# Residual additions inside the next stage, two weight units fed per chunk, and sums of squares in three column tiles

## The reference

```python
h = x
f = _swiglu(_rmsnorm(h, ffn1_pre_g), ...)
h = h + 0.5 * _rmsnorm(f, ffn1_post_g)
u = _rmsnorm(h, mix_pre_g)
c_q, c_kv, k_pe, rw, gates = split(u @ w_in)
...                                   # attention and RWKV-7, merged into mix
h = h + _rmsnorm(mix @ w_out, mix_post_g)
f = _swiglu(_rmsnorm(h, ffn2_pre_g), ...)
h = h + 0.5 * _rmsnorm(f, ffn2_post_g)
gp = sigmoid(_rmsnorm(h, ple_pre_g) @ w_ple_gate)
h = h + _rmsnorm(gp * (pemb @ w_ple_proj), ple_post_g)
```

## Time and profile before

| | |
|---|---|
| median of three runs | 3861.78 us (3854.52 to 3871.53) |
| the profiled execution | 3863.07 us, of which the span of the trace is 3861.3 us |
| TensorE products busy | 3430.6 us, 89% of the span |
| VectorE, ScalarE, GpSimd busy | 1695.9, 929.8, 440.8 us |
| mean granted TensorE clock | 0.932 of full speed |

### The profile page before, as it was taken

One profiled execution on the slowest core, in us unless ns is written; L12 is line 12 of the kernel. 1 busy time (PEld: TensorE's weight loads), 2 busy tenths in 40 slices (PEclk: granted clock), 3 DMA queues, 4 the chain that ended last, 5 costly groups with the idle time before them and its releaser, 6 DMA issues. The chain is left out here.

```text
span 3861.3 us, 69674 instructions
## 1 busy us (share of the span) xinstructions
PE 3430.6 (89%) x28907; PEld 3086.5 (80%) x28907; DVE 1695.9 (44%) x2998; ACT 929.8 (24%) x1610; POOL 440.8 (11%) x457
## 2 busy tenths in 40 slices
PE   7999999969999799889994888869869999999776
PEld 6999999959999637766662767659859999999766
DVE  3343343353121245345444777755154443343443
ACT  3111111121000105434441333333221111111131
POOL 0000000020000000033331344420010000000212
PEclk9999999979999898989996899979979999999878
DMA  2011111122222300056552011023121111111122
GB/s 102 34 55 45 50 39 45 44 107 75 91 94 94 110 2 13 16 206 208 191 192 60 14 31 31 12 95 117 67 83 50 50 50 33 50 50 39 75 80 97
DMA packets 114583, 279.64 MB, mean 72 GB/s; under 512 B 45428, under 2 KB 56500, under 8 KB 113236
## 3 DMA queue, kind: packets, MB, share of 16 engines
q1 hardware_dynamic: 95860, 199.87, 15.4%
q0 software_dynamic: 18432, 75.51, 5.6%
HBM read 231.41 MB, written 43.80 MB: 71 GB/s over the span
## 5 line engine op out<-in xcount | busy, mean ns | idle before, releaser
L79 PE MATMUL f_psg<-f_u_hi,f_w_hi 128*128 128x352 f32 x1056 | 347.1, 329 | 62.7 <-DVE f_w_lo L336 58.2
L428 DVE TENSOR_TENSOR c_x<-c_x,f_psd 128x352 f32<-128x352 f32 x480 | 246.2, 519 | 318.0 <-PE f_psd L81 318.0
L79 PE MATMUL f_psd<-f_hid_hi,f_w_hi 128*128 128x352 f32 x1056 | 350.3, 332 | 18.2 <-DVE c_x L428 9.8
L332 ACT ACTIVATE f_w_hi<-f_raw 128x1024 fp32r<-128x1024 f32 x132 | 136.6, 1054 | 915.7 <-PE f_psd L81 352.3
L79 PE MATMUL f_psu<-f_u_hi,f_w_hi 128*128 128x352 f32 x1056 | 342.5, 324 | 5.5 <-DVE f_w_lo L336 5.5
L80 PE MATMUL f_psg<-f_u_lo,f_w_hi 128*128 128x352 f32 x1056 | 342.7, 325 | 0.0
L81 PE MATMUL f_psg<-f_u_hi,f_w_lo 128*128 128x352 f32 x1056 | 342.5, 324 | 0.0
L80 PE MATMUL f_psd<-f_hid_lo,f_w_hi 128*128 128x352 f32 x1056 | 341.6, 324 | 0.0
L81 PE MATMUL f_psd<-f_hid_hi,f_w_lo 128*128 128x352 f32 x1056 | 341.3, 323 | 0.0
L80 PE MATMUL f_psu<-f_u_lo,f_w_hi 128*128 128x352 f32 x1056 | 340.2, 322 | 0.0
L81 PE MATMUL f_psu<-f_u_hi,f_w_lo 128*128 128x352 f32 x1056 | 339.8, 322 | 0.0
(11 more groups left out here) (391 smaller groups left out, 7226.3 us busy)
## 6 DMA issues: line engine op xcount, KB each, us to landing
f_raw<-in_ffn_gu SPq DMA_DIRECT2D x88, 512.0 KB, 4.3
f_raw<-in_ffn_d SPq DMA_DIRECT2D x44, 512.0 KB, 4.0
proj<-in_out SPq DMA_DIRECT2D x36, 528.0 KB, 2.9
inw_raw<-in_w_in_units SPq DMA_DIRECT2D x36, 512.0 KB, 3.9
h<-c_x SPq DMA_DIRECT2D x24, 528.0 KB, 2.7
r_old<-h SPq DMA_DIRECT2D x3, 4224.0 KB, 12.9
c_x<-proj SPq DMA_DIRECT2D x16, 528.0 KB, 4.5
mgw_raw<-in_merge_units SPq DMA_DIRECT2D x16, 512.0 KB, 4.7
```

What stands on the lines that cost most here:

```text
L79: pe.matmul(out, w_hi, x_hi, start=start, stop=False)
L332: act.activation(w_hi[:, u % 3, :], raw[:, u % 3, :], ACT.Copy).then_inc(hi_done, 1)
L428: dve.tensor_tensor(a, a, ps_d[:, n % 2, 0:TB], ALU.add).then_inc(added, 1)
```

## The change

The stages r1, r2 and r3 are gone. What they did is written into the beginning of the stage that follows (`Residual`, `WideNorm`); r4 stays as `last_residual_phase`.

- **Old h by chunk.** SP loads old h in chunks of 528 KB into a ring of three buffers, stores chunk c of the sum when it is added, and loads chunk c + 3 behind that store. In f2 and in the input projection the first two weight units are loaded ahead of this, in the embedding unit 0.
- **By chunk on VectorE**: scale chunk c + 1 (and add old h, for chunks 0, 2, 4, 6, 7; in the embedding 0, 1, 2, 4, 6, 7), then u_lo of chunk c. GpSimd adds the others.
- **Two units per chunk.** In f1, f2 and the input projection TensorE takes, for each chunk, the 9 products of unit 0 and the 9 of unit 1 into six banks. In the embedding it takes the three blocks of unit 0 per chunk, after the products with p for these blocks.
- **Sums of squares.** In the five norms of f1, in, f2, pl and r2's squares, each chunk's squares go from ScalarE to TensorE, which multiplies them with 32 columns of ones, one token block to each of three column tiles (output partitions 0, 32, 64). The residual norms whose squares were summed before have one such product of `n_total`. The root and the reciprocal are then 96 x 352, and each block's row is spread by a product with a contraction of one.

The diff, cut to its core:

```diff
+class WideNorm:
+    def act_square(self, act, x, c):
+        wait(act, self.sq_summed, c - 1)
+        act.activation(self.buf.sq[:, c % 2, :], x[:, c, :], ACT.Square).then_inc(self.sq_ready, 1)
+    def pe_sum(self, pe, bank, c):
+        pe.wait_ge(self.sq_ready, c + 1)
+        for b in range(NTB):
+            mm = pe.matmul(bank[32 * b:32 * (b + 1), 0:TB], self.env.ones[:, 0:32],
+                           self.buf.sq[:, c % 2, token_block(b)], start=c == 0, stop=c == KC - 1)
+        mm.then_inc(self.sq_summed, 1)
...
+    def pe_spread(self, pe, banks):
+        pe.wait_ge(self.rs_ready, 1)
+        for b in range(NTB):
+            if b >= len(banks):
+                pe.wait_ge(self.rb_ready, b - len(banks) + 1)
+            pe.matmul(banks[b % len(banks)][:, 0:TB], self.env.ones[32 * b:32 * b + 1, :],
+                      self.buf.rs[32 * b:32 * b + 1, :], start=True, stop=True).then_inc(self.spread, 1)
...
+class Residual:
+    RING = 3
...
+    def sp_all(self, sp):
+        for c in range(self.RING):
+            self.sp_load(sp, c)
+        for c in range(KC):
+            self.sp_store(sp, c)
+            if c + self.RING < KC:
+                self.sp_load(sp, c + self.RING)
...
 def ffn_phase(...):                   # ScalarE
+            split_hi(act, 0, 0)
+            for c in range(KC):
+                x_in(act, c)
+                act_hi(act, x, g_col, u_hi, c, u_hi_ready)
+                if c == 0:
+                    split_hi(act, 0, 1)
+                norm.act_square(act, x, c)
             norm.act_root(act, ps_d[:, 1, :])
             norm.act_rb(act, nbanks)
...
 def input_projection_phase(...):      # VectorE
+            res.dve_gain(dve)
+            res_norm.dve_reciprocal(dve)
+            dve.wait_ge(res_norm.rb_ready, NTB)
+            res.dve_scale(dve, 0, buf.rb[:, :])
+            wu.split_lo(dve, 0, 0)
+            for c in range(KC):
+                if c < KC - 1:
+                    res.dve_scale(dve, c + 1, buf.rb[:, :])
+                res.wait_chunk(dve, c)
+                dve_lo(dve, x, g_col, u_hi, u_lo, c, u_hi_ready, u_lo_ready)
+                if c == 0:
+                    wu.split_lo(dve, 0, 1)
+            norm.dve_reciprocal(dve)
...
 def embedding_phase(...):             # ScalarE, then TensorE
+            res_norm.act_root(act, psn[:, 1, :])
+            res_norm.act_rb(act, nbanks)
+            act.wait_ge(p_in, 16)
+            act.activation(p_hi[:, :, :], pe_in[:, :, :], ACT.Copy).then_inc(p_hi_ready, 1)
+            wu.split_hi(act, 0, 0)
...
+            wu.ready(pe, 0, 0)
+            pe.wait_ge(p_lo_ready, 1)
+            for b in range(NTB):
+                wu.product(pe, ps[:, b, 1, 0:TB], 0, KC, PC, p_hi, p_lo, token_block(b))
...
-def residual_phase(nc, env, name, x, g_col, coef, res, h_out, buf, stored, summed, last=False):
+def last_residual_phase(nc, env, name, x, g_col, coef, res, h_out, buf, stored):
-        BY_POOL = (0, 2, 4, 6)
+        BY_POOL = (1, 3, 5)
-            sp.dma_start(old[:, :, :], res).then_inc(old_in, 16)
             for c in range(KC):
+                sp.dma_start(old[:, c, :], res[:, c, :]).then_inc(old_in[c], 16)
...
-            norm.pe_sums(pe, ps_sum)
-            norm.pe_spread_all(pe, ps_rb)
+            norm.pe_total(pe, ps_sum)
+            norm.pe_spread(pe, [ps_rb[:, b, :] for b in range(NTB)])
```

More of the change, by code:

```diff
@@ L387, in _ @@
         def _(dve):
[L388 to L392, removed]
+            if res is not None:
+                res.dve_gain(dve)
+                res_norm.dve_reciprocal(dve)
+                dve.wait_ge(res_norm.rb_ready, NTB)
+                res.dve_scale(dve, 0, buf.rb[:, :])
+            split_lo(dve, 0, 0)
+            for c in range(KC):
+                if res is not None and c < KC - 1:
+                    res.dve_scale(dve, c + 1, buf.rb[:, :])
+                x_in(dve, c)
+                dve_lo(dve, x, g_col, u_hi, u_lo, c, u_hi_ready, u_lo_ready)
+                if c == 0:
+                    split_lo(dve, 0, 1)
+            norm.dve_reciprocal(dve)
+            rb3 = buf.rb[:, :].rearrange("p (b t) -> p b t", b=NTB)
             def gate_evac(s, j):
@@ L559, in ready, with product @@
         pe.wait_ge(self.lo_done, i * 2 + (k + 1))
-    def product(self, pe, out, k, first, chunks, x_hi, x_lo, tokens, x_ready=None):
+    def product(self, pe, out, k, first, chunks, x_hi, x_lo, tokens):
         for c in range(chunks):
-            if x_ready is not None:
-                pe.wait_ge(x_ready, c + 1)
             w = slice((first + c) * P, (first + c + 1) * P)
@@ L615, in _ @@
                 sp.wait_ge(stored[k], 16 * (N_IN // 2))
-            sp.wait_ge(*reading)
+            sp.wait_ge(res.stored, 16 * KC)
+        @block.gpsimd
+        def _(pool):
+            res.pool_adds(pool)
         @block.scalar
         def _(act):
[L620 to L623, removed]
+            res_norm.act_root(act, psn[:, 1, :])
+            res_norm.act_rb(act, nbanks)
+            wu.split_hi(act, 0, 0)
+            for c in range(KC):
+                res.wait_chunk(act, c)
+                act_hi(act, x, g_col, u_hi, c, u_hi_ready)
+                if c == 0:
+                    wu.split_hi(act, 0, 1)
+                norm.act_square(act, x, c)
             norm.act_root(act, psn[:, 1, :])
@@ L631, in _ @@
         def _(dve):
[L632 to L637, removed]
+            res.dve_gain(dve)
+            res_norm.dve_reciprocal(dve)
+            dve.wait_ge(res_norm.rb_ready, NTB)
+            res.dve_scale(dve, 0, buf.rb[:, :])
+            wu.split_lo(dve, 0, 0)
+            for c in range(KC):
+                if c < KC - 1:
+                    res.dve_scale(dve, c + 1, buf.rb[:, :])
+                res.wait_chunk(dve, c)
+                dve_lo(dve, x, g_col, u_hi, u_lo, c, u_hi_ready, u_lo_ready)
+                if c == 0:
+                    wu.split_lo(dve, 0, 1)
+            norm.dve_reciprocal(dve)
+            dve.wait_ge(norm.rb_ready, NTB)
             def evac(i, k):
```

320 lines of the change are left out of this document (226 added, 94 removed).

## The result

The changed kernel takes 3803.73 us, the median of four runs (3791.69 to 3810.84), against 3860.45 for the kernel before (four runs, 3854.52 to 3871.53): a ratio of 0.9847, with an interval of 0.9811 to 0.9883. The forecast was 3801, with a range of 3780 to 3842. The profiled execution took 3798.92, its span 3797.1; the mean granted clock rose from 0.932 to 0.944.

The account below looks back on a forecast made before the run. TensorE bounds the kernel, its longest waits at stage starts. Savings of 19.1 (input projection), 16.2 (FFN 2), 1.2 (FFN 1), 21.9 (embedding) and 4.0 (r4) sum to 62.4, taking 3863.07 to 3801 us; range 3780 to 3842.

Parts of the forecast that it names:

- the chunk: Input projection, clock at full: 18 products and a sum of squares every 3.55 us.
- the 74 in 11.40: Profile row behind the full-clock price of a 352-column product: 74 products in 11.40 us, 0.154 each.
- drain between tiling modes: TensorE drains when tiling changes; once more per chunk, 24 chunks would add 3.4 us; left out of the sum.
- The rival of tiles one after another: Column tiles do not overlap, each sum of squares takes 2.85 or 4.05 us: 3884 us in all; chance 0.05.
- Spreading: Norms' spreading by TensorE: same 2112 pass columns, 4.05 or 2.85 us, with the last copy 4.6 or 3.4.
- Input projection and embedding: Starts of these two stages: 19.1 us saved in the input projection, 21.9 in the embedding.
- the rival I gave 0.13: VectorE and GpSimd share something: VectorE operations of fed stretches take 1.46 times as long, 3821 us; chance 0.13.
- the 3.4 of slack: Input projection: VectorE's last u_lo comes 3.4 us before TensorE wants it.
- a sign of being wrong: Chunks every 5 us, TensorE waiting for u_lo within f2's chunks, or a gap beyond 10 us behind the last chunk.
- f2: FFN 2 with r2: sums at the half clock, first product at 2813.3, unit 2 in effect at 2855.0; 16.2 us saved.
- FFN 1: No residual here: products start at 15.0, unit 2 in effect at 56.7 instead of 57.9; 1.2 us saved.
- What hides it: Input projection and f2: products hide the scaling, adding and stores moved into the stages.

Follow-up runs that it names:

- one_tile: The changed kernel with a sum's three products in one column tile instead of three and the spreads read from one row group: 3839.14 us.

## Why the prediction was right

**The mechanism.** The waits shrank as described, and the gain is of the size forecast: 64.0 against 62.4 in the stages. The terms missed by up to 3.0 in both directions, so part of that agreement is luck.

- *Prices.* A sum in three tiles came out at 0.79 (0.78), the reciprocal at 2.35 (2.1), the chunk at 3.79 (3.55). A product costs 0.159, not 0.154: the 74 in 11.40 count the products that the window's ends cut, which is 0.09 of a chunk. FFN 1's chunk less 18 x 0.159 leaves 0.93 for a sum, with what follows it: 0.15 more per chunk, 3.6 over 24 chunks, though only FFN 1's eight are paced by TensorE. The Trainium skill's drain between tiling modes ("TensorEngine Tiling (Array Packing)", Key Properties), which I had priced at 3.4 and left out of the sum, would stand here, and the trace agrees with it: two sums with no change of tiling between them last 1.38, so the second costs 0.59, where one between full products costs 0.93. No run separates the drain from anything else that a change of product costs. The rival of tiles one after another is the run one_tile: 35 us more, and still faster than before.
- *Spreading* was the wrongest price: the same pass columns as before, I said, so 2.85 to 4.05. A product with a contraction of one runs beside its neighbour in another row group: 0.86 for two, 1.55 for r4's three at the half clock. That is r4's 6.9 instead of 4.0: scaling started 6.2 after the barrier, not 8.7. In the other stages, with two banks, the third spread waits for a copy, and the whole with the last copy took 4.1 and 2.8 instead of 4.6 and 3.4.
- *Input projection and embedding* fell short by 2.1 and 3.0 through the rival I gave 0.13, in another form than I priced it. I read the 10.90 of six u_lo beside p_lo as a slowdown by half of everything; it was one instruction that stood, 4.75 for the first of the six. What I set against this rival, that scaling kept its 1.25 beside r1's additions, did not carry over: r1 read the norm from PSUM (`r_rb`), the change reads a copy of it in SBUF (`n_rb`). In the input projection the standing ate the 3.4 of slack: the eight chunks took 35.5 us, and 35.4 in f2 (31.8 were forecast; FFN 1 took 32.0). With that a sign of being wrong came true, in a small form: TensorE waits for u_lo within f2's chunks, 0.4 to 0.8 at a time. In the embedding the weights' low part took 5.53, and it stands ahead of the first chunk, where I had put p_lo's cost among the u_lo. The u_lo of the kernel before, and the low part in the change:

```profile
3683.42 4.75 DVE L226 SCALAR_TENSOR_TENSOR pl_u_lo<-c_x,c_gains,pl_u_hi 128x1056 fp32r<-128x1056 f32 x1 [3.29 <-ACT pl_u_hi L223]
...
3614.52 5.53 DVE L741 TENSOR_TENSOR plw_lo<-plw_raw,plw_hi 128x1280 fp32r<-128x1280 f32 x1 [0.33 <-ACT plw_hi L737]
```

- *f2* gained 1.4 more than forecast, because r2's eight sums did not all run at the half clock. Four took 0.79 each, as at the full clock; the four between them took 4.55 together (24 passes, granted clock 0.64). They were done 9.8 after the barrier, not 13.7, and TensorE started at 23.7, not 27.6; VectorE's pace took most of that back.

```profile
2771.86 0.79 PE L251 MATMUL f_psd<-n_sq,c_ones 128*32 128x352 f32 x6 [2.41 <-ACT n_sq L246]
2772.83 4.55 PE L251 MATMUL f_psd<-n_sq,c_ones 128*32 128x352 f32 x24 [0.18 <-ACT n_sq L246]
```

- *FFN 1* gained 3.7, not 1.2: TensorE started at 14.1, not 15.0, and stood 6.4 behind the last chunk, not 7.4.
- *What hides it* held for the stores and loads: TensorE waits for no transfer within the chunks.

**What the sum did not have.** The 9.2 of the two shifted stages. No step of mine asked where a new tile puts the tiles behind it. With it the stages come to 54.8, and the medians differ by 56.7. The two profiled executions differ by 64.2: f2's unchanged part was 7.9 shorter in this pair, the stretch from the loop's end to r2 1.9 shorter and FFN 1 behind unit 2's gate 0.4 longer, which closes the account. Most of the 7.9 is waiting: in f2's unchanged part TensorE waited for a weight's low part 10.5 us in the kernel before,

```profile
PE f_psg L79 <- DVE f_w_lo L336: 10.5, 4, 2.8
```

against the 4.9 shown above for the change. Whether the kernel before always does, its one profile cannot say; the medians fit scatter (54.8 of their 56.7). That the forecast of 3801 met 3804 is luck in part: 9.2 were left out, and against that the terms came out 1.6 better, the execution it counts from stood 2.6 above the median of four, and 1.9 of the medians' difference are in no term.

## What to carry to other kernels

Feeding a stage chunk by chunk took 17 to 19 us out of each of the three boundaries here, but behind the last chunk the norm's chain is bare: where TensorE sets the pace, hold back products that need nothing new until it is over. Adding on GpSimd was no offload here while VectorE read two operands from SBUF: look for instructions that last as long as the other engine's. After a change that adds a tile, compare the pitch of products in code that did not change.

## What the runs showed that was not expected

- A product of 128 x 352 follows the one before after 0.159 us when its weights and moving data begin at multiples of 128 bytes (counted as above), 0.160 with weights at 64 past one, 0.162 with weights or, in FFN 2's gate and up products, moving data at 32: up to 2% of a stage that TensorE bounds.
- Products of one row in different row groups run side by side: 0.86 us for two, 0.85 for one.
- One ScalarE instruction of 0.55 us does what root and reciprocal did in 0.55 and 2.35.
